# Projection slabs stepped in among attention tiles, and two attention runs joined, in a three-layer transformer kernel

## The chip, the cores and the metric

The kernel runs on one core of a Trainium2 chip. The metric is the device time of one execution in microseconds (us). TensorE (PE) does the matrix products, VectorE (DVE), ScalarE (ACT) and GpSimd (POOL) work on 128 partitions, SyncE (SP) issues the weight loads. PSUM, the memory into which TensorE writes, has eight banks of 128 x 512 fp32 values.

## The reference, cut to what matters

512 tokens, width 1024, three layers in a row. Each layer is: norm, input projection, two mixers side by side of width 512, output projection, norm, gated FFN of width 2816.

```
layer 1: q,k,v, glu_a,glu_g = norm(x) @ w_in
         attn = block attention, 8 heads of 64, with a position bias     ("moba")
         conv = silu(layernorm(causal depthwise conv, 31 taps, of glu_a*sigmoid(glu_g)))
layer 2: fox:  8 heads of 64, logits + (c_q - c_k), c = cumsum(log_sigmoid(forget gate))
         diff: 4 heads of 128, softmax(q1 k1) - lambda * softmax(q2 k2), then an RMS norm per head
         q1,q2,k1,k2 of diff carry a partial rotary embedding
layer 3: latent ("dsa"): 8 heads, keys and values from a rank-128 latent; only the 128 keys of the
         largest index score count for a query (top-k)
         stick-breaking ("sb"): weights sigmoid(z) * product of sigmoid(-z) of later keys
x = x + concat(mixers) @ w_out;  x = x + ffn(norm(x));  after each layer's blocks a next norm
```

## The kernel before, in words

Everything is held transposed: features on partitions, 512 tokens along the row. Weights come in slabs of 128 x 2048 (a 1024 x 256 piece of a matrix), one load of 1 MB each into one of two slots `raw`, in one fixed order over the whole program; `BASE[phase]` is the number of a phase's first slab. Each slab is split into a high and a low part: ScalarE casts `w_hi` from `raw` (line 734), VectorE subtracts (`w_lo`, line 1075). TensorE multiplies each slab with the activations' parts `a_hi` and `a_lo` in three products: 48 matmuls of 512 columns for a feature slab (lines 368 to 370, 256 features), or 96 of 256 columns for a token slab (lines 381 to 383, values with tokens on partitions). The result stands in a pair of PSUM banks, pairs 0-1 and 2-3 in turn. `split(n + 2)` is done one slab ahead of its use.

Each engine has its own instruction list, written by hand in the order in which it runs; semaphores with counts tie them together (`wait("slab", n)` and so on). Nothing reorders them.

An attention stage consists of tiles: `Unit` u is one pair of heads (or one diff head) and one block of 128 queries `qt` (0 to 3), whose width is `u.w` = 128, 256, 384 or 512 keys. Layer 1 has 16 tiles, layers 2 and 3 have 32 (diff then fox; sb then dsa). `attend` on each engine runs rounds i, with the scores three tiles ahead (`AHEAD = 3`):

- TensorE (line 560): `scores(run[i+3])` (line 501) into a PSUM pair, `turn(run[i])` (transposes, line 520, banks 4 and 5), `values(run[i-1])` (line 537, banks 6 and 7 in turn by group of four tiles). Four `rotate` pairs and the root transposes `token_rows` stand in layer 2's projection.
- VectorE: `taken(run[i+3])` (line 1306) reads scores from PSUM, adds mask or bias and finds the row maximum; `factors(run[i+2])` (lines 1326 to 1337) scales by 1/sum; then spare work (`taps` of the convolution, line 1252, in layer 1; `top_rounds` in layer 3); then the eviction of a finished group (`a_lo`, line 1362). For sb tiles it is two scans (line 1315) and products (line 1320) in place of both.
- ScalarE: `exps(run[i+3])` (line 881), `move(run[i])` (line 903) copies the transposes out of PSUM, then the eviction's high part (`a_hi`, line 933) and the diff head's norm (lines 926 to 948).
- GpSimd, for fox only: adds the decay row to a tile's mask (lines 334 and 338), two tiles ahead.

Scores use two PSUM pairs in turn by the tile's number, so `scores(u)` waits for `taken` of the tile two before. All slabs of an input projection (10, 13, 11 in the three layers) are finished before a layer's `attend` begins, since the scores use the same banks. In layer 3 `attend` is called twice, for sb and for dsa; the masks of the chosen keys (lines 1610 and 1612) are made between them. In layer 1, VectorE does ten taps per projection slab from the fifth on (3 before the split, 7 behind it) and three per tile; 124 in all, which the layer norm's sums on TensorE (line 595) wait for.

Of the kernel before, what the change touches and what calls it, by code (L numbers as in the profile page):

```python
# [29 lines left out]
P = 128  # L30
S = 512
# [111 lines left out]

def runs_of(t):

    return [UNITS[t][i:i + 16] for i in range(0, len(UNITS[t]), 16)]
# [28 lines left out]
def build(nc, weights, vectors, x_in, positions, bias_rows, buckets, uk, uv,  # L175
# [4 lines left out]
    with ctx:  # L180
# [48 lines left out]
        fg = tmp[0:HEADS, 1:4, :]  # L229
# [17 lines left out]
        def lane_scores(u, lane):  # L247
            return ps[:, 2 * (u.n % 2) + lane, 0:u.w]
# [100 lines left out]
        def _(pe):  # L349
# [106 lines left out]
            def token_rows():  # L456

                for t in range(QT):
                    m = pe.transpose(ps[:, 6, t * P:(t + 1) * P], tmp[:, 5, t * P:(t + 1) * P], ident)
                m.then_inc(sem["rtok_mm"], 1)  # L460
# [29 lines left out]
            def scores(u):  # L490
                q = slice(u.qt * P, (u.qt + 1) * P)
                if u.n >= 2:
                    wait("taken", 2 * (u.n - 1))
                for lane in range(2):
# [28 lines left out]
            def values(u):  # L523
                wait("pt", 2 * u.n + 2)
                if u.first and u.group >= 2:
                    wait("oev", u.group - 1)
                q = slice(u.qt * P, (u.qt + 1) * P)
# [55 lines left out]
            for j in range(10):  # L583
                project("in1", j, in_fill("norm0") if j == 0 else None, tokens=j >= 8)
# [5 lines left out]
            wait("qkv", 6)  # L590
            attend(runs_of(1)[0])
# [32 lines left out]
            for j in range(1, 6):  # L624
                project("in2", j)
            wait("r23_dve", 2)
            wait("lam_act", 1)
            token_rows()
            wait("fg_dve", 4)
            for t in range(QT):  # L630
                m = pe.transpose(ps[:, 7, t * 8:t * 8 + 8], fg[:, 1, t * P:(t + 1) * P],
                                 sq_f[0:HEADS, 1, 0:HEADS])
            m.then_inc(sem["cq_mm"], 1)
            for j in range(6, 10):
                project("in2", j, tokens=j >= 9)
                for r in (2 * (j - 6), 2 * (j - 6) + 1):
                    wait("qkv", QKV["in2"] + j)
                    rotate(2, r, 8 + r)
            for j in range(10, 13):
                project("in2", j, tokens=True)  # L640
            wait("qkv", QKV["in2"] + 13)
            wait("rope", 8)
            wait("cq_ev", 1)
            attend(UNITS[2])
# [27 lines left out]
            token_rows()  # L672
# [40 lines left out]
            attend(runs_of(3)[0])  # L713
            attend(runs_of(3)[1])
# [6 lines left out]
        def _(act):  # L721
# [183 lines left out]

            def out_chunk(u):
# [3 lines left out]
            def attend(run):  # L910
                n, kind = len(run), run[0].kind
                ends = {i: u for i, u in enumerate(run) if u.last}
                for i in range(-AHEAD, n + 6):
                    a = i + AHEAD
                    if a < n:
                        if run[a].kind == "sb":
                            sticks(run[a])
                        else:
                            exps(run[a])
                    norms = {k: ends[i - k] for k in (2, 4, 6) if i - k in ends and ends[i - k].kind == "diff"}  # L920
                    if 4 in norms:
                        u = norms[4]
                        wait("df_sum", u.p + 1)
                        if u.p:
                            wait("alo", LOWS["att2"] + u.p)
                        A.activation(tmp[:, 1, :], ps[:, BT + 1, :], ACT.Ln, bias=col("eps"),
# [3 lines left out]
                    if i - 2 in ends and ends[i - 2].kind != "diff":  # L930
                        u = ends[i - 2]
                        wait("pv", u.n + 1)
                        A.copy(a_hi[:, out_chunk(u), :], ps[:, BO + u.group % 2, :]).then_inc(sem["ahi"], 1)
                    if 2 in norms:
                        u = norms[2]
                        wait("pv", u.n + 1)
                        if u.p:
                            wait("df_sum", u.p)
                        A.activation(tmp[:, 0, :], ps[:, BO + u.group % 2, :], ACT.Square
                                     ).then_inc(sem["df_sq"], 1)  # L940
                    if 4 in norms:
                        u = norms[4]
                        wait("df_ln", u.p + 1)
                        A.activation(tmp[:, 1, :], tmp[:, 1, :], ACT.Exp, scale=-0.5).then_inc(sem["df_root"], 1)
                    if 6 in norms:
                        u = norms[6]
                        wait("oev", u.group + 1)
                        A.copy(a_hi[:, out_chunk(u), :], tmp[:, 1, :]).then_inc(sem["ahi"], 1)
# [805 lines left out]
```

## Time and profile before

| | |
|---|---|
| median of 3 runs | 1937.97 us (1933.84 to 1938.27) |
| the profiled execution | 1936.62 us |
| its span, from the first to the last instruction | 1934.8 us |
| TensorE busy | 1834.5 us, 95% |
| VectorE, ScalarE, GpSimd busy | 1107.6, 753.6, 113.4 us |
| mean granted TensorE clock | 0.978 |
| moved from HBM | 163.10 MB, 85 GB/s over the span |

A clock of 1.00 is 2.4 GHz, 0.50 is 1.2 GHz; in between a stretch had both. A window row gives a stretch in us from the span's start, and in it each engine's busy time. A timeline row gives start, duration, engine, line, operation, tensors, and in brackets how long the engine was idle before it and what ended that. `x10` at the end of such a row means ten instructions merged, the time from the first's start to the last's end. PEld is the loading of the stationary operand, beside PE.

### The profile page before, as it was taken

To read this page: it belongs to the slowest core of one execution; us is meant where nothing else is said; L and a number is where in the kernel's file an instruction comes from. 1 tells how busy PE (TensorE), PEld (TensorE's weight loads), DVE (VectorE), ACT (ScalarE), POOL (GpSimd) and SP (SyncE) were. 2 spreads that over 40 slices of the span, in tenths; PEclk is the share of its full clock that TensorE was granted. 3 is DMA by queue.
4 is the path that set the end of the run, shared out by engine and by line. 5 is a ranking of instruction groups with operands and counts; after the bars stand their busy time and mean duration, and the time that the engine had idled before them with its cause. 6 is when DMAs were issued, how large, how long until landed. Compare 5 with 4: busy or idle time off the path is not lost.

```text
span 1934.8 us, 23475 instructions
## 1 busy us (share of the span) xinstructions
PE 1834.5 (95%) x8886; PEld 1466.6 (76%) x8886; DVE 1107.6 (57%) x1664; ACT 753.6 (39%) x1089; POOL 113.4 (6%) x114
## 2 busy tenths in 40 slices
PE   5987999999999999879999999999978999999998
PEld 4874788888887888448888888887755788888886
DVE  5889454444333454853667673347997366676422
ACT  4225443333323211663454442222257354445321
POOL 0000010000011000261000000100000010000000
PEclk9997999999999999889999999999989999999999
DMA  4430122223233422001322223332210123232221
GB/s 156 149 108 2 32 100 93 102 88 107 87 109 109 145 90 78 16 1 66 105 91 94 101 89 106 109 119 75 78 44 1 44 88 108 87 103 92 100 96 65
DMA packets 25719, 166.24 MB, mean 86 GB/s; under 512 B 3082, under 2 KB 3210, under 8 KB 6704
## 3 DMA queue, kind: packets, MB, share of 16 engines
q1 hardware_dynamic: 23328, 158.83, 23.8%
q0 software_dynamic: 1744, 5.37, 0.9%
q8 instruction: 50, 0.82, 0.2%
q10 hardware_dynamic: 576, 1.05, 0.2%
q14 instruction: 21, 0.17, 0.0%
HBM read 163.10 MB, written 2.13 MB: 85 GB/s over the span
## 4 chain that ended last, share of the span: by engine, by line
PE 88%; DVE 6%; issue 2%; ACT 2%; POOL 1%; DMA 0%; DVEq 0%; SPq 0%; ACTq 0%
PE ps L368 25%; PE ps L369 25%; PE ps L370 25%; PE ps L383 2%; PE ps L382 2%; PE ps L381 2%; PE ps L520 1%; PE ps L537 1%; DVE cacc L1252 1%; ACT ring L881 1%; DVE ring L1306 1%; PE ps L501 1%; POOL tmp L334 1%; PE ps L486 1%; DVE tmp L1315 1%
## 5 line engine op out<-in xcount | busy, mean ns | idle before, releaser
L368 PE MATMUL ps<-a_hi,w_hi 128*128 128x512 f32 x1616 | 635.3, 393 | 7.4 <-DVE a_lo L1081 3.8
L370 PE MATMUL ps<-a_hi,w_lo 128*128 128x512 f32 x1616 | 629.7, 390 | 0.0
L369 PE MATMUL ps<-a_lo,w_hi 128*128 128x512 f32 x1616 | 629.5, 390 | 0.0
L368 PEld LDWEIGHTS ps<-a_hi,w_hi 128*128 128x128 f32 x1616 | 303.9, 188 | 76.8 <-issue 9.8
L369 PEld LDWEIGHTS ps<-a_lo,w_hi 128*128 128x128 f32 x1616 | 304.0, 188 | 64.8 <-issue 2.6
L370 PEld LDWEIGHTS ps<-a_hi,w_lo 128*128 128x128 f32 x1616 | 303.8, 188 | 63.8
L1075 DVE TENSOR_TENSOR w_lo<-raw,w_hi 128x2048 fp32r<-128x2048 f32 x82 | 192.3, 2345 | 244.1 <-ACT w_hi L734 244.0
L734 ACT CAST w_hi<-raw 128x2048 fp32r<-128x2048 f32 x82 | 156.0, 1903 | 417.0 <-PE ps L370 335.1
L368 PE MATMUL ps<-h_hi,w_hi 128*128 128x512 f32 x528 | 206.2, 391 | 0.0
L370 PE MATMUL ps<-h_hi,w_lo 128*128 128x512 f32 x528 | 205.4, 389 | 0.0
L369 PE MATMUL ps<-h_lo,w_hi 128*128 128x512 f32 x528 | 205.4, 389 | 0.0
L1169 DVE TENSOR_TENSOR tmp<-ps,tmp 128x512 f32<-128x512 f32 x66 | 45.7, 692 | 175.1 <-PE ps L370 158.2
L1220 DVE SCALAR_TENSOR_TENSOR tmp<-tmp,vec 128x510 f32<-128x510 f32 (+1 forms) x176 | 120.0, 745 | 0.0
L369 PEld LDWEIGHTS ps<-h_lo,w_hi 128*128 128x128 f32 x528 | 99.1, 188 | 21.1 <-issue 0.5
L368 PEld LDWEIGHTS ps<-h_hi,w_hi 128*128 128x128 f32 x528 | 99.1, 188 | 20.9 <-issue 0.5
L370 PEld LDWEIGHTS ps<-h_hi,w_lo 128*128 128x128 f32 x528 | 99.1, 188 | 20.6
L1209 DVE TENSOR_TENSOR w_lo<-raw,w_hi 128x2048 fp32r<-128x2048 f32 x44 | 100.9, 2293 | 21.6 <-ACT w_hi L858 19.7
L520 PE MATMUL ps<-sq_f,ring 128*128 128x128 f32 x360 | 66.8, 317 | 46.8 <-ACT pT L903 32.4
L520 PEld LDWEIGHTS ps<-sq_f,ring 128*128 128x128 f32 x360 | 45.6, 160 | 84.7 <-DVE ring L1331 44.5
L858 ACT CAST w_hi<-raw 128x2048 fp32r<-128x2048 f32 x44 | 84.2, 1914 | 47.0 <-PE ps L370 47.0
L881 ACT ACTIVATE ring<-ring,stat 128x128 f32<-128x128 f32 (+3 forms) x128 | 70.8, 554 | 70.7 <-DVE stat L1306 70.6
L501 PE MATMUL ps<-qk 64*128 64x128 f32 (+3 forms) x320 | 75.5, 560 | 16.3 <-DVE stat L1306 9.5
(207 smaller groups left out, 1962.5 us busy)
## 6 DMA issues: line engine op xcount, KB each, us to landing
raw<-weights_dram SPq DMA_DIRECT2D x148, 1024.0 KB, 4.9
bias_t<-bias_rows_scratch POOLq DMA_DIRECT2D x8, 256.0 KB, 7.3
ncb<-decay_rows_scratch POOLq DMA_DIRECT2D x8, 256.0 KB, 4.7
out_dram<-xT SPq DMA_DIRECT2D x8, 256.0 KB, 2.0
xT<-x_in_dram ACTq DMA_DIRECT2D x4, 256.0 KB, 6.2
xT<-x_in_dram SPq DMA_DIRECT2D x4, 256.0 KB, 9.1
vec<-vectors_dram SPq DMA_DIRECT2D x1, 282.5 KB, 3.6
ring<-ramp_dram POOLq DMA_DIRECT2D x1, 260.0 KB, 5.4
```

The costliest lines, as they stand in the source:

```text
L368: pe.matmul(dst, wh, hi[:, k0 + k, :], start=start and k == 0, stop=False)
L369: pe.matmul(dst, wh, lo[:, k0 + k, :], start=False, stop=False)
L370: last = pe.matmul(dst, wl, hi[:, k0 + k, :], start=False, stop=stop and k == nk - 1)
L501: m = pe.matmul(lane_scores(u, lane), qq, kk, start=True, stop=u.kind != "sb")
L520: m = pe.transpose(ps[:, BT + lane, b * P:(b + 1) * P], e[:, b * P:(b + 1) * P], ident)
L734: A.copy(w_hi[:, n % 2, :], raw[:, n % 2, :]).then_inc(sem["whi"], 1)
L858: A.copy(w_hi[:, n % 2, :], raw[:, n % 2, :]).then_inc(sem["whi"], 1)
L881: A.activation(e, e, ACT.Exp, bias=stat[:, slot, 0:1], scale=-1.0, accum_out=stat[:, slot, 1:2]).then_inc(sem["ex"], 1)
L1075: Vv.tensor_tensor(w_lo[:, n % 2, :], raw[:, n % 2, :], w_hi[:, n % 2, :].bitcast(F32), ALU.subtract).then_inc(sem["wlo"], 1)
L1169: Vv.tensor_tensor(tmp[:, first, :], ps[:, bank + first, :], tmp[:, 5, :], ALU.mult).then_inc(sem["evg"], 1)
L1209: Vv.tensor_tensor(w_lo[:, n % 2, :], raw[:, n % 2, :], w_hi[:, n % 2, :].bitcast(F32), ALU.subtract).then_inc(sem["wlo"], 1)
L1220: step = Vv.scalar_tensor_tensor(out=to, in0=tmp[:, g, 0:S - lag], scalar=w, in1=to, op0=ALU.mult, op1=ALU.add)
```

## The change

The last three slabs of layer 1's input projection (numbers 7, 8, 9) and the last seven of layer 2's (6 to 12) are no longer done ahead of the attention but in steps of an eighth of a slab, `filler`, two (at two places three) in each round of TensorE's `attend`, between `scores` and `turn`, from round -3 on: to round 8 in layer 1, to round 23 in layer 2. Slabs are put in another order, so that what the first tiles need comes first (values with heads 0 to 3 of layer 1 as slab 6; in layer 2 diff before fox). The steps write into PSUM pair 2-3; as long as they do, and for the tiles whose scores are made then (`shared`), scores have only pair 0-1, so `scores(u)` waits for `taken` of the tile just before. A finished filler slab is moved out of PSUM, and the slab two further is split, in the round in which its last step stands (`FILLED`: rounds 0, 4, 8; in layer 2 also 12, 16, 20, 23). Because the steps still read the activations `a_hi` and `a_lo`, the finished attention groups may not be written there until round 9 (layer 1) or 24 (layer 2); diff results are parked in qk2 chunks 8 to 11 and copied in rounds 26, 27, 28 and 30. Layer 1 has ten taps fewer at each of three slabs and four in place of three per tile, the rest behind the last eviction. In layer 3 both runs become one `attend(UNITS[3])`: the masks and ScalarE's table load stand ahead of the first dsa tile's `taken` and `exps`.

```diff
+def filler_steps():
+    plan, step = {}, 0
+    for i in range(-AHEAD, 24):
+        count = 2 if i < 21 or i == 23 else 3
+        plan[i] = [(6 + (step + k) // 8, (step + k) % 8) for k in range(count)]
+        step += count
+    return plan
+STEPS = filler_steps()
+FILLED = {i: steps[-1][0] for i, steps in STEPS.items() if steps[-1][1] == 7}
+TOKENS = {"in1": (6, 9), "in2": (5, 6, 9, 12)}
+STEPS1 = {i: [(7 + k // 8, k % 8) for k in (2 * (i + AHEAD), 2 * (i + AHEAD) + 1)] for i in range(-AHEAD, 9)}
+FILLED1 = {i: steps[-1][0] for i, steps in STEPS1.items() if steps[-1][1] == 7}
+ALONE1 = 10 + AHEAD
+ALONE = 16 + 24 + AHEAD
+LATER = {26: 0, 27: 1, 28: 2, 30: 3}
...
-        fg = tmp[0:HEADS, 1:4, :]
+        fg = tmp[0:HEADS, 2:5, :]
+        r23 = tmp[:, 1, :]
...
-            return ps[:, 2 * (u.n % 2) + lane, 0:u.w]
+            pair = 0 if shared(u) else u.n % 2
+            return ps[:, 2 * pair + lane, 0:u.w]
+        def shared(u):
+            return u.n < {1: ALONE1, 2: ALONE, 3: 0}[u.t]
+        def evicted(run, i):
+            hold = {1: 9, 2: 24, 3: 0}[run[0].t]
+            return [u for k, u in enumerate(run) if u.last and u.kind != "diff" and max(k + 2, hold) == i]
...
             def scores(u):
                 q = slice(u.qt * P, (u.qt + 1) * P)
-                if u.n >= 2:
+                if u.n >= 1 and shared(u):
+                    wait("taken", 2 * u.n)
+                elif u.n >= 2:
                     wait("taken", 2 * (u.n - 1))
...
+            def filler(name, j, step):
+                n = BASE[name] + j
+                if step == 0:
+                    wait("wlo", n + 1)
+                    wait("qkv", QKV[name] + j - (4 if name == "in1" else 0))
+                if j not in TOKENS[name]:
+                    last = feature_major(n % 2, 2, a_hi, a_lo, step, 1, step == 0, step == DC - 1, at=step)
+                else:
+                    t, dst = step // 2, ps[:, 2 + step // 4, (step // 2 % 2) * 256:(step // 2 % 2) * 256 + 256]
+                    for k in range(step % 2 * 4, step % 2 * 4 + 4):
...
+                if step == 7:
+                    last.then_inc(sem["slab"], 1)
-            def attend(run):
+            def attend(run, steps={}):
                 n, kind = len(run), run[0].kind
                 for i in range(-AHEAD, n + 4):
                     if i + AHEAD < n:
                         scores(run[i + AHEAD])
+                    for j, step in steps.get(i, ()):
+                        filler(f"in{run[0].t}", j, step)
                     if 0 <= i < n:
                         turn(run[i])
...
-            for j in range(10):
-                project("in1", j, in_fill("norm0") if j == 0 else None, tokens=j >= 8)
+            for j in range(7):
+                project("in1", j, in_fill("norm0") if j == 0 else None, tokens=j >= 6)
...
-            wait("qkv", 6)
-            attend(runs_of(1)[0])
+            attend(UNITS[1], STEPS1)
...
-            attend(UNITS[2])
+            attend(UNITS[2], STEPS)
...
-            attend(runs_of(3)[0])
-            attend(runs_of(3)[1])
+            attend(UNITS[3])
...
@@ ScalarE, attend @@
                     if 0 <= i < n:
                         move(run[i])
-                    if i - 2 in ends and ends[i - 2].kind != "diff":
-                        u = ends[i - 2]
+                    if i in filled and run[0].t == 1:
+                        move_first(filled[i], 1)
+                    if i in filled:
+                        split(BASE[f"in{run[0].t}"] + filled[i] + 2)
+                    for u in evicted(run, i):
...
@@ VectorE @@
+            def filled_slab(j):
+                if j in TOKENS["in2"]:
+                    move_tokens("in2", j, v2, {6: 768, 9: 0, 12: 256}[j], pair=1)
+                else:
+                    c = {7: 0, 8: 4, 10: 2, 11: 6}[j]
+                    move_features("in2", j, qk2[:, c:c + 2, :], SCALE if c < 4 else 1.0, pair=1)
+                split(BASE["in2"] + j + 2)
...
                     if a < n and run[a].kind != "sb":
+                        if run[a] is runs_of(3)[1][0]:
+                            latent_masks()
                         taken(run[a])
...
                         spare()
-                    if i - 2 in ends and ends[i - 2].kind != "diff":
-                        u = ends[i - 2]
+                    if i in filled and run[0].t == 2:
+                        filled_slab(filled[i])
+                    elif i in filled:
+                        split(BASE["in1"] + filled[i] + 2)
+                    for u in evicted(run, i):
...
-            attend(runs_of(1)[0], lambda: taps(3))
+            attend(UNITS[1], lambda: taps(4), FILLED1)
+            taps(4 * TAPS)
...
-                if 1 <= j <= DC:
-                    c = j - 1
+                for c in range(2 * j - 2, 2 * j) if 1 <= j < 5 else ():
                     Vv.scalar_tensor_tensor(out=xT[:, c, :], in0=xT[:, c, :], scalar=col("gain", DC * 2 + c),
                                             in1=tmp[:, 0, :], op0=ALU.mult, op1=ALU.mult).then_inc(sem["x"], 1)
```

## Rows read from the trace of the kernel before

**Rows 1.** The page, 40 equal slices: TensorE's granted clock in tenths

```profile
PEclk9997999999999999889999999999989999999999
```

**Rows 2.** Windows: the attentions of layers 1, 2 and 3 (two runs)

```profile
core 0: us, PE busy (x) PEld busy (x) DVE busy (x) ACT busy (x) POOL busy (x), PEclk, DMA share, GB/s
...
136.40:203.06 66.66, 45.39 (x306) 28.39 (x305) 58.84 (x160) 35.32 (x102) 0.00 (x0) 0.77 0.05 17
...
767.05:871.00 103.95, 77.37 (x497) 47.21 (x497) 74.29 (x238) 66.84 (x198) 42.15 (x42) 0.87 0.03 11
...
1412.90:1467.95 55.05, 42.35 (x337) 25.00 (x337) 52.14 (x105) 38.33 (x101) 0.00 (x0) 0.88 0.06 20
...
1467.95:1514.65 46.70, 37.58 (x306) 23.19 (x304) 30.69 (x121) 33.77 (x103) 0.00 (x0) 0.93 0.01 1
```

**Rows 3.** Windows: dense slabs; four diff tiles; four latent tiles

```profile
300.00:320.00 20.00, 20.00 (x90) 16.57 (x89) 9.05 (x9) 6.71 (x7) 0.00 (x0) 1.00 0.30 105
...
797.94:808.16 10.22, 8.14 (x49) 4.89 (x48) 8.42 (x29) 7.81 (x23) 0.00 (x0) 1.00 0.01 2
...
1488.58:1498.70 10.12, 8.62 (x79) 5.43 (x77) 7.21 (x30) 7.62 (x26) 0.00 (x0) 1.00 0.00 1
```

**Rows 4.** Timeline of VectorE, layer 1

```profile
129.22 6.71 DVE L1252 SCALAR_TENSOR_TENSOR cacc<-cu,vec,cacc 128x512 f32<-128x512 f32 x10
...
138.53 2.29 DVE L1075 TENSOR_TENSOR w_lo<-raw,w_hi 128x2048 fp32r<-128x2048 f32 x1 [2.59 <-ACT w_hi L734]
...
163.74 0.68 DVE L1306 CUSTOM_DVE_ANT_0 ring<-ps,bias_t 128x512 f32<-128x512 f32 x1
...
203.79 0.69 DVE L1362 TENSOR_TENSOR a_lo<-ps,a_hi 128x512 fp32r<-128x512 f32 x1 [5.11 <-ACT a_hi L933]
```

**Rows 5.** Timeline of ScalarE and TensorE, layer 1

```profile
102.69 1.91 ACT L734 CAST w_hi<-raw 128x2048 fp32r<-128x2048 f32 x1 [8.04 <-PE ps L370]
...
136.60 1.90 ACT L734 CAST w_hi<-raw 128x2048 fp32r<-128x2048 f32 x1 [8.70 <-PE ps L383]
...
138.40 1.01 ACT L986 COPY v<-ps 128x1024 f32<-128x1024 f32 x1
...
145.93 3.36 PE L501 MATMUL ps<-qk 64*128 64x384 f32 x8 [5.02 <-DVE stat L1306]
...
203.06 3.70 PE L595 MATMUL ps<-cacc,sq_f 128*128 128x512 f32 x8
```

**Rows 6.** Windows: start of layer 1's attention

```profile
140.00:150.00 10.00, 4.98 (x18) 1.82 (x16) 9.57 (x29) 3.88 (x13) 0.00 (x0) 0.50 0.31 105
```

**Rows 7.** Timeline of VectorE (slab moves) and TensorE, layer 2

```profile
680.40 1.22 DVE L1264 SCALAR_TENSOR_TENSOR qk<-ps,tmp 128x1024 f32<-128x1024 f32 x1 [5.93 <-PE ps L370]
...
704.96 1.23 DVE L1264 SCALAR_TENSOR_TENSOR qk<-ps,tmp 128x1024 f32<-128x1024 f32 x1 [3.72 <-PE ps L370]
...
767.09 1.23 DVE L1271 TENSOR_TENSOR v<-ps,small 128x1024 f32<-128x1024 f32 x1 [7.24 <-PE ps L383]
...
771.84 3.36 PE L501 MATMUL ps<-qk 64*128 64x384 f32 x8 [2.55 <-DVE stat L1306]
```

**Rows 8.** Timeline of VectorE, GpSimd and TensorE, layer 2's second half

```profile
822.10 1.72 DVE L1331 TENSOR_SCALAR ring<-ring,stat 128x512 f32<-128x512 f32 x2
...
844.32 3.14 POOL L334 TENSOR_SCALAR tmp<-ncb,cq_t 128x512 f32<-128x512 f32 x2
...
847.25 1.13 PE L501 MATMUL ps<-qk 64*128 64x512 f32 x4
...
862.68 0.88 DVE L1331 TENSOR_SCALAR ring<-ring,stat 128x512 f32<-128x512 f32 x2
...
870.96 0.50 PE L368 MATMUL ps<-a_hi,w_hi 128*128 128x512 f32 x1 [1.41 <-DVE a_lo L1362]
```

**Rows 9.** Timeline between layer 3's two runs

```profile
1468.67 1.28 ACT L1055 ACT_TABLE_LOAD   x1
...
1468.68 0.69 DVE L1362 TENSOR_TENSOR a_lo<-ps,a_hi 128x512 fp32r<-128x512 f32 x1 [2.54 <-ACT a_hi L933]
...
1470.76 3.24 PE L501 MATMUL ps<-qk 64*128 64x384 f32 x8 [1.88 <-DVE stat L1306]
```

More of the change, by code:

```diff
@@ L491, in scores @@
                 q = slice(u.qt * P, (u.qt + 1) * P)
-                if u.n >= 2:
+                if u.n >= 1 and shared(u):
+                    wait("taken", 2 * u.n)
+                elif u.n >= 2:
                     wait("taken", 2 * (u.n - 1))
+                if u.kind == "diff" and u.first:
+                    wait("rope", 5 + u.p)
+                if u.kind == "fox" and u.first and u.p % 2 == 0:
+                    wait("qkv", QKV["in2"] + (9 if u.p == 0 else 12))
+                if u.t == 1 and u.n in (0, 8, ALONE1):
+                    wait("qkv", {0: 3, 8: 5, ALONE1: 6}[u.n])
+                if u.t == 2 and u.n == ALONE:
+                    wait("qkv", QKV["in2"] + 13)
                 for lane in range(2):
@@ L526, in values @@
                     wait("oev", u.group - 1)
+                if u.t == 1 and u.m == 8:
+                    wait("qkv", 6)
+                if u.t == 2 and u.first and u.p % 2 == 0:
+                    j = {"diff": (6, 7), "fox": (10, 13)}[u.kind][u.p // 2]
+                    wait("qkv", QKV["in2"] + j)
+                if u.kind == "diff" and u.m == 0:
+                    wait("rtok", 1)
+                    wait("cq_ev", 1)
                 q = slice(u.qt * P, (u.qt + 1) * P)
@@ L904, in move, with move_first, attend @@
                            ).then_inc(sem["pt"], 2 if diff else 1)
+            def move_first(j, pair):
+                wait("slab", BASE["in1"] + j + 1)
+                bank = ps[:, 2 * pair:2 * pair + 2, :]
+                if j in TOKENS["in1"]:
+                    c = 0 if j == 6 else 256
+                    A.copy(v1[:, :, c:c + 256], bank.rearrange("p b (t c) -> p (b t) c", c=256)
+                           ).then_inc(sem["qkv"], 1)
+                else:
+                    c = {4: 0, 5: 4, 7: 2, 8: 6}[j]
+                    A.activation(qk1[:, c:c + 2, :], bank, ACT.Copy, scale=SCALE if c < 4 else 1.0
+                                 ).then_inc(sem["qkv"], 1)
             def out_chunk(u):
                 return (4 if u.kind in ("diff", "sb") else 0) + u.p
-            def attend(run):
+            def attend(run, filled={}):
                 n, kind = len(run), run[0].kind
@@ L918, in attend @@
                         else:
+                            if run[a] is runs_of(3)[1][0]:
+                                act.preload_act_table_set("natural_log_exp_and_others")
                             exps(run[a])
-                    norms = {k: ends[i - k] for k in (2, 4, 6) if i - k in ends and ends[i - k].kind == "diff"}
+                    norms = {k: ends[i - k] for k in (2, 4) if i - k in ends and ends[i - k].kind == "diff"}
                     if 4 in norms:
@@ L1414, in _ @@
             wait("rope_act", 3)
-            for j in range(10):
+            for j in range(7):
                 o = PAIR["in1"] + j
@@ L1462, in _ @@
             wait("lam_dve", 3)
[L1463 removed]
+            for j in range(6):
                 n, o = BASE["in2"] + j, PAIR["in2"] + j
```

151 lines of the change are left out of this document (71 added, 80 removed).

## The prediction

> **What bounds the kernel now.** I read the clock row of the page first. TensorE's granted clock is 10 tenths nearly everywhere and dips in three places [rows 1]; these are the three attention stages. The dense stages can't be moved: 90 matmuls fill 20.00 us completely at clock 1.00, 0.222 us each [rows 3], so a slab of 48 costs 10.7 us, and nothing but less work shortens it. A token slab (96 matmuls of half the width) is 11.5: from the cast behind slab 6 to that behind slab 9 are 33.9 us, one feature slab and two of these [rows 5].
>
> Then the windows of the attention stages. In layer 1 TensorE is busy 45.4 of 66.7 us at clock 0.77, in layer 2 77.4 of 104.0 at 0.87 [rows 2]. In layer 1 the bound is VectorE, 58.8 of 66.7 us: it does the convolution's taps between the tiles. In layer 2 nobody is full (DVE 74, ACT 67, POOL 42 of 104): a stage of waits. Four tiles cost TensorE 8.1 us (diff) or 8.6 (two lanes; the latent tiles stand for fox) where the clock is 1.00, and VectorE 8.4 and 7.2 [rows 3]. At full clock the 32 tiles of layer 2 are 4 x 8.1 + 4 x 8.6 = 67 us of TensorE, so some 37 of its 104 are idle or lost to the clock; in layer 1 16 tiles are 34, so 32 of 66.7. That is what slabs could fill.
>
> **Layer 1: three slabs (7, 8, 9) go among the tiles.** TensorE's work is only moved. With them go 3 weight splits (2.2 us of VectorE, 1.9 of ScalarE each), three moves out of PSUM (1.0 of ScalarE) and 30 taps of 0.66 us [rows 4, 5], since each projection step carried ten taps. VectorE is the bound, and its work is moved, not removed:
> - Slab 6 is now a token slab and ends 0.8 later, at 103.4. VectorE comes to the first tile 9.0 later, as before (cast 1.9, split 2.2, seven taps 4.6; TensorE's 5.02 us of idleness ending at 145.93 is this [rows 5]): 112.4.
> - Its work until the last tap: 58.8 in the stage, less 2.3 and seven taps (4.6) ahead of the tiles, makes 51.9. Plus 30 taps 19.9 and three splits 6.6: 78.4 [rows 2, 4].
> - Waits. Scores now have one PSUM pair, so each scores() waits for the tile just before, and TensorE puts two filler steps (2.7) between two scores: VectorE starves in the first three rounds, whose own work is 3.4 us in all, by 5.0. In a filled round the split waits for tile, move and cast on ScalarE: scores 1.1 + steps 2.7 + transpose 0.4 + copy 0.4 + move 1.0 + cast 1.9 = 7.5 after the round's start, while VectorE is done at 5.8: 1.7, then less, 4 for three. Together 9.
> - 112.4 + 78.4 + 9 = 199.8, where TensorE began the layer norm's sums at 203.06: 3 earlier. But three taps now stand behind the last eviction, and TensorE has waited some 7 us; before, after idle stretches of 3.0 and 5.0 us, the clock was 0.50 over the ten us [rows 6], with 3.4 us for scores that cost half of it at full clock [rows 5]. I charge 2 for the restart. **Layer 1: -1.** Ends: no waits -10, double waits +8.
>
> In filler rounds both engines are full: VectorE 27.3/4 + sixteen taps 10.6 + split 2.2 = 19.6 per four tiles, TensorE 8.6 + 10.7 = 19.3. So little can be caught up.
>
> **Layer 2: seven slabs (6 to 12) go among 27 rounds.**
> - Slab 5 ended at 680.4 [rows 7]. It is now a token slab (+0.6, a slab with its handing over being 10.9) with the root transposes and three rotation pairs ahead; transposes and one pair cost 24.6 - 2 x 10.9 = 2.8 [rows 7], two more pairs some 3.4: 687.2. A last pair: 688.9. The attention began at 767.1: 78 earlier.
> - Start-up: scores and two steps to 692.2. VectorE is free at 695.7 (behind slab 5: move 1.2, wait 0.8, split 2.2, two ropes 4.0, copy 0.2). Two more rounds of scores and steps, 7.7: 703.4. The clock falls after such a pause [rows 6], 3 more: round 0 begins at 706.5.
> - Rounds 0 to 23 at full clock: 50 steps (two token slabs but for six steps, a third) 68.6; tiles 4 x 8.1 + 2 x 8.6 + 1.0 = 50.8; in the seven filled rounds the next but one scores() waits for VectorE, which stands behind ScalarE's cast: taken() at 9.7 where TensorE comes at 8.6, 1.1 each, 7.7. Sum 127: 833.6. VectorE has only 8.4 + 3.4 of 19 us, so this part is TensorE's, and busy shares of 8.1 in 10.2 us kept the clock at 1.00 [rows 3].
> - Splits now run beside GpSimd's decay tiles (3.14 for two at full width), where two scalings by VectorE took 1.72 instead of 0.88 [rows 8]. No split ran beside them before: between 0 and one GpSimd instruction, 1.6, for each of four; nearest is the scaling's 0.8, on less than all: +2, 835.6.
> - Tail: from the scores of tile 27 (847.25) to the next projection (870.96) 23.7 [rows 8]; the held-back evictions (six pairs of 0.6 on each of ScalarE and VectorE) add 1.5 (0 to 4): 860.8.
> - At nothing: the residual's scaling, now two per step, and the ropes moved two slabs forward fit into VectorE's 5.93 idle us per slab [rows 7]; another tile for the roots, and the diff results parked in freed chunks of qk2, move no work. The weight loads keep their order on SP's queue and wait for the splits; with 20 us between splits in place of 11 none is late. Without that cover the scaling would cost 0.7 more per slab.
> - **Layer 2: -10.** Ends: without the waits, slow clock, contention and evictions -24; with them doubled +4.
>
> On the contention the Trainium skill ("SBUF — State Buffer", Who interferes with whom) says that a VectorE instruction with two SBUF inputs and a GpSimd one that reads SBUF exclude each other, and the split is of that kind. By it each of the four splits is held for up to a whole GpSimd instruction, which would make the +2 a +6; the 1.72 beside 0.88 agrees in kind.
>
> **Layer 3: one pipeline.** TensorE's last stick values ended at 1467.95; then 2.54 us of VectorE idleness, a table load of 1.28, 1.88 idle on TensorE and 3.24 for scores at half clock [rows 9]. Merged, scores and transposes of the latent tiles begin earlier, but VectorE's bound remains until its last scan (52.1 of 55.1 us busy [rows 2]), the masks (1.0) and the table load move ahead of ScalarE's copies of the last three stick tiles, and these hold up the transposes: by my walk through the rounds only 1 us, and 1.5 of slow clock. **-2.5**, ends 0 and -5. The order of the tail is as before.
>
> **Sum.** -1 - 10 - 2.5 = -13.5 against the profiled execution, 1936.6 us (span 1934.8 and 1.8 around it); it lies 1.4 below the median shown. 1936.6 - 13.5 = 1923.1, by the median 1924.5: **1924**.
>
> **Rivals.**
> - *The waits are absorbed* (VectorE catches up, the rounds overlap). For it: tiles run three rounds ahead, layer 2's VectorE has seven idle us in nineteen. Against: one score pair allows one round of slack. The free ends sum to -10 - 24 - 5 = -39, **1899**; anything below 1912 counts here.
> - *The clock.* Short pauses in every round keep it as low as in the stage before, 0.87. TensorE's 119 us of rounds 0 to 23 grow by 0.15, 18: **1942**, no change. For it: 0.77 and 0.87 [rows 2]; against: 0.80 busy at 1.00 [rows 3]. The Trainium skill ("TensorE: Matmul & The Clock Gate", A second HAM failure mode: psum-queue depth-cycling) says that short pauses between groups as PSUM banks are cycled make the clock swing; this rival is that rule.
> - *The steps hide nothing*: TensorE works in order, the steps stand ahead of transposes and values, and a tile's chain grows by all of it. Then the 78 and 33 us saved ahead are given back: **1938**. Against: the transposes have two rounds of slack.
> - *Slower: the single score pair.* Scores, taken() and the next scores become one chain, 0.7 + 0.8 + 0.3 of handing over = 1.8 us in each round where VectorE is a round late. Eight of the 39 rounds eat the 13.5; from twelve on it is slower. In layer 1's twelve and the seven filled of layer 2: 19 x 1.8 = 34, **1958**. For it: layer 1's VectorE is full. Against: behind the scores lie 2.7 us of steps for taken() to hide in.
>
> **Chances.** Forecast 0.60 (own range 1912 to 1932), absorbed 0.17, clock 0.09, hides nothing 0.07, slower 0.07. The range takes in both no-change cases, 1938 and 1942, and leaves out half of "absorbed" below (0.085), "slower" (0.07) and a little of the clock's case above: 1908 to 1942. 0.3%, 5.8 us, is about what a measurement of this kernel can tell from no change: faster (below 1932.2) 0.77, same 0.16, slower 0.07.
>
> **What would show it.** Layer 1: first scores near 106.5; VectorE without gaps but for about 5 us at the start and 1 to 2 at w_hi in filled rounds; a TensorE pause of about 7 before the layer norm's sums near 200. Layer 2: first scores near 689 instead of 768; about 5 us per filled round, clock 1.00 from 710 on; the output projection near 861. Layer 3: stretch 1412.9 to 1514.65, 101.8, down to about 99. Wrong I am if the clock dips in the rounds, if a split waits several us in the fox half, or if TensorE's pauses in layer 1 are not at the two ends.

## The result, and the profile after

The changed kernel takes 1924.1 us (median of 4, 1922.8 to 1925.7) where the kernel before took 1937.97; the ratio is 0.9934, with a 95% interval of 0.9916 to 0.9951. Forecast were 1924, in 1912 to 1932 for its own case. The total is right, but partly by luck: layer 1 came out 3.2 us worse than forecast and layer 2 3.0 better, and the two cancel. By the profiled executions (span 1934.8 before), with the start of each output projection as the mark:

| stage | before | after | measured | forecast |
|---|---|---|---|---|
| to layer 1's output projection | 206.19 | 208.37 | +2.2 | -1 |
| from there to layer 2's | 664.77 | 651.59 | -13.2 | -10 |
| from there to layer 3's | 643.69 | 641.23 | -2.5 | -2.5 |

The page after: span, busy time of each engine, and the granted clock in 40 slices, the row that answers to [rows 1].

```profile
span 1921.4 us, 23482 instructions
...
PE 1827.2 (95%) x8886; PEld 1461.7 (76%) x8886; DVE 1104.5 (57%) x1664; ACT 754.9 (39%) x1089; POOL 114.5 (6%) x114
...
PEclk9998899999999999989999999999989999999999
```

The three dips of the clock are narrower but still there. The windows show where; they answer to [rows 2]: the tiles of layer 1 with the three slabs among them, its layer norm sums, rounds 0 to 23 of layer 2, its tail, and three pieces of layer 3.

```profile
core 0: us, PE busy (x) PEld busy (x) DVE busy (x) ACT busy (x) POOL busy (x), PEclk, DMA share, GB/s
112.60:203.08 90.48, 67.98 (x481) 49.83 (x481) 78.95 (x182) 40.06 (x106) 0.00 (x0) 0.91 0.10 36
203.08:208.37 5.29, 5.29 (x8) 2.23 (x9) 0.00 (x0) 0.00 (x0) 0.00 (x0) 0.59 0.00 0
...
707.47:830.39 122.92, 119.21 (x737) 91.95 (x737) 70.21 (x185) 58.20 (x147) 33.36 (x33) 1.00 0.16 52
830.39:859.96 29.57, 20.48 (x159) 13.47 (x157) 18.51 (x47) 18.52 (x46) 9.89 (x9) 0.83 0.11 36
...
1401.92:1456.97 55.05, 42.52 (x312) 24.70 (x312) 53.95 (x116) 38.53 (x103) 0.00 (x0) 0.84 0.06 20
1456.97:1475.00 18.03, 14.49 (x132) 9.19 (x130) 12.91 (x55) 14.14 (x48) 0.00 (x0) 1.00 0.00 1
1475.00:1501.19 26.19, 21.32 (x202) 13.95 (x198) 15.74 (x57) 18.86 (x55) 0.00 (x0) 1.00 0.01 2
```

Layer 2's rounds are what the change is for: TensorE is busy 119.2 of 122.9 us at clock 1.00. The tail behind them is worse than before, 29.6 us at 0.83 where [rows 8] gave 23.7. In layer 1 VectorE is busy 79.0 of 90.5 us, and TensorE does its sums at clock 0.59.

The timeline of VectorE and TensorE in layer 1 (start, duration, and in brackets the idle time before and who ended it):

```profile
106.02 0.80 PE L542 MATMUL ps<-qk 64*128 64x128 f32 x4 [2.96 <-ACT v L975]
112.49 0.70 PE L542 MATMUL ps<-qk 64*128 64x256 f32 x4 [0.36 <-DVE stat L1378]
113.23 0.42 DVE L1378 CUSTOM_DVE_ANT_0 ring<-ps,bias_t 128x256 f32<-128x256 f32 x1 [0.79 <-PE ps L542]
117.02 0.56 DVE L1378 CUSTOM_DVE_ANT_0 ring<-ps,bias_t 128x384 f32<-128x384 f32 x1 [2.42 <-PE ps L542]
121.04 0.69 DVE L1378 CUSTOM_DVE_ANT_0 ring<-ps,bias_t 128x512 f32<-128x512 f32 x1 [2.25 <-PE ps L542]
127.31 2.29 DVE L1147 TENSOR_TENSOR w_lo<-raw,w_hi 128x2048 fp32r<-128x2048 f32 x1 [1.45 <-ACT w_hi L797]
147.87 2.29 DVE L1147 TENSOR_TENSOR w_lo<-raw,w_hi 128x2048 fp32r<-128x2048 f32 x1 [1.20 <-ACT w_hi L797]
168.76 2.29 DVE L1147 TENSOR_TENSOR w_lo<-raw,w_hi 128x2048 fp32r<-128x2048 f32 x1 [1.49 <-ACT w_hi L797]
177.81 0.42 DVE L1378 CUSTOM_DVE_ANT_0 ring<-ps,bias_t 128x256 f32<-128x256 f32 x1 [1.49 <-PE ps L542]
...
195.06 5.38 DVE L1324 SCALAR_TENSOR_TENSOR cacc<-cu,vec,cacc 128x512 f32<-128x512 f32 x8
200.35 0.69 DVE L1448 TENSOR_TENSOR a_lo<-ps,a_hi 128x512 fp32r<-128x512 f32 x1
200.95 2.07 DVE L1324 SCALAR_TENSOR_TENSOR cacc<-cu,vec,cacc 128x512 f32<-128x512 f32 x3
203.08 5.86 PE L664 MATMUL ps<-cacc,sq_f 128*128 128x512 f32 x8 [8.56 <-DVE cacc L1324]
```

First scores at 106.0 (forecast 106.5). VectorE starves for 0.79 + 2.42 + 2.25 = 5.5 us in the three start-up rounds (forecast 5.0) and waits 1.2 to 1.5 for each cast, 4.1 in three (forecast 4). Eleven taps stand at the end, three of them behind the last eviction; TensorE waits 8.56 us for them and then takes 5.86 us for sums that took 3.70 in [rows 5].

The same for layer 2, with two of TensorE's short pauses in filled rounds (behind `taken()`, and behind VectorE's normalised result, which frees a bank for the values), GpSimd around one split, and the end of the filled rounds:

```profile
691.04 0.49 PE L542 MATMUL ps<-qk 64*128 64x128 f32 x4
...
698.40 0.70 PE L542 MATMUL ps<-qk 64*128 64x256 f32 x4 [3.81 <-DVE stat L1378]
...
735.19 0.70 PE L542 MATMUL ps<-qk 64*128 64x256 f32 x4 [0.23 <-DVE stat L1378]
...
775.10 0.46 PE L586 MATMUL ps<-pT,v 128*128 128x128 f32 x2 [0.82 <-DVE qk L1453]
...
790.43 0.67 POOL L369 TENSOR_TENSOR tmp<-tmp,causal 128x256 f32<-128x256 f32 x1
792.18 2.29 DVE L1147 TENSOR_TENSOR w_lo<-raw,w_hi 128x2048 fp32r<-128x2048 f32 x1 [1.21 <-ACT w_hi L797]
...
795.65 1.53 POOL L365 TENSOR_SCALAR tmp<-ncb,cq_t 128x384 f32<-128x384 f32 x1 [4.54 <-DVE stat L1378]
...
832.22 2.29 DVE L1147 TENSOR_TENSOR w_lo<-raw,w_hi 128x2048 fp32r<-128x2048 f32 x1 [2.17 <-ACT w_hi L797]
835.15 0.72 ACT L944 ACTIVATE ring<-ring,stat 128x512 f32<-128x512 f32 x1 [2.97 <-DVE stat L1378]
836.97 1.09 PE L561 MATMUL ps<-sq_f,ring 128*128 128x128 f32 x4 [3.63 <-ACT pT L966]
...
859.96 0.50 PE L399 MATMUL ps<-a_hi,w_hi 128*128 128x512 f32 x1 [1.41 <-DVE a_lo L1448]
```

The attention starts at 691.0, which is the forecast 688.9 plus the 2.2 that layer 1 lost. The last split (832.22) belongs to the seventh slab and feeds the second slab of the output projection, which TensorE reaches some 36 us later (859.96 and a slab of 10.7). It waits 2.17 us for ScalarE and runs 2.29. Behind it come the tile's `taken()`, ScalarE's exponential (2.97 idle) and TensorE (3.63 idle); from 835.5 to 842.3 the clock is at half (1.09 us for four transposes that take 0.63 at full clock).

### The profile page after: what moved, and what is told of

It reads as the page before. It is cut to its first block, busy times and chain, and to the rows that moved or that the text cites. A ratio compares the mean times of both kernels' runs of the same rounds, so it can differ in the third digit from the quotient of the medians.

```text
span 1921.4 us, 23482 instructions
## 1 busy us (share of the span) xinstructions
PE 1827.2 (95%) x8886; PEld 1461.7 (76%) x8886; DVE 1104.5 (57%) x1664; ACT 754.9 (39%) x1089; POOL 114.5 (6%) x114
## 4 chain that ended last, share of the span: by engine, by line
PE 88%; DVE 5%; ACT 3%; issue 3%; DMA 0%; DVEq 0%; SPq 0%; ACTq 0%
PE ps L399 25%; PE ps L401 25%; PE ps L400 25%; PE ps L542 2%; PE ps L561 1%; DVE cacc L1324 1%; PE ps L586 1%; ACT w_hi L797 1%; PE ps L622 1%; ACT ring L944 1%; PE ps L414 1%; PE ps L413 1%; PE ps L412 1%; PE ps L623 1%; PE ps L624 1%
## 5 line engine op out<-in xcount | busy, mean ns | idle before, releaser
L944 ACT ACTIVATE ring<-ring,stat 128x128 f32<-128x128 f32 (+3 forms) x128 | 71.0, 556 | 119.2 <-DVE stat L1378 119.2
L399 PEld LDWEIGHTS ps<-h_hi,w_hi 128*128 128x128 f32 x528 | 99.1, 188 | 21.1 <-issue 0.5
L400 PEld LDWEIGHTS ps<-h_lo,w_hi 128*128 128x128 f32 x528 | 99.1, 188 | 21.0 <-issue 0.5
L401 PEld LDWEIGHTS ps<-h_hi,w_lo 128*128 128x128 f32 x528 | 99.1, 188 | 20.6
L934 ACT ACTIVATE tmp<-tmp 128x512 f32<-128x512 f32 x44 | 27.8, 632 | 157.7 <-DVE tmp L1292 157.7
L339 POOL TENSOR_TENSOR tmp<-tmp 128x512 f32<-128x512 f32 x28 | 36.8, 1316 | 872.7 <-ACT tmp L810 871.0
L561 PE MATMUL ps<-sq_f,ring 128*128 128x128 f32 x360 | 59.6, 295 | 28.0 <-ACT pT L966 21.2
```

The source lines that it names most:

```text
L399: pe.matmul(dst, wh, hi[:, k0 + k, :], start=start and k == 0, stop=False)
L400: pe.matmul(dst, wh, lo[:, k0 + k, :], start=False, stop=False)
L401: last = pe.matmul(dst, wl, hi[:, k0 + k, :], start=False, stop=stop and k == nk - 1)
L561: m = pe.transpose(ps[:, BT + lane, b * P:(b + 1) * P], e[:, b * P:(b + 1) * P], ident)
L944: A.activation(e, e, ACT.Exp, bias=stat[:, slot, 0:1], scale=-1.0, accum_out=stat[:, slot, 1:2]).then_inc(sem["ex"], 1)
```

## The experiments

Eleven kernels ran in four groups, each beside runs of the kernel before (medians 1936.9 to 1937.4 us). Edits are to the changed kernel unless said; `...` marks lines left out. Times of whole kernels are medians; marks, windows and waits come from one profiled execution each.

One thing limits what a single mark tells. Behind the same pause TensorE's half clock can begin and end at another place in another execution. Layer 1's output projection, 208.37 in the changed kernel, stands at 209.31 in u_l3 and 210.57 in e_defer, whose layer 1 is the same code. In e_defer the start-up's half clock lasted from 110.8 to 117.7 us, in the changed kernel from 105.1 to 111.9, and VectorE's longest wait for scores in the start-up was 4.59 us in place of 2.42. A difference of 2 us at this mark is within the scatter of equal code.

**One part undone: layer 1** (u_l1). All ten slabs come ahead of the tiles; the slab loops of all three engines change alike, and the first scores wait for the last key slab.

```
-STEPS1 = {i: [...] for i in range(-AHEAD, 9)}
+STEPS1 = {}
...
-ALONE1 = 10 + AHEAD
+ALONE1 = 0
...
-            hold = {1: 9, 2: 24, 3: 0}[run[0].t]
+            hold = {1: 0, 2: 24, 3: 0}[run[0].t]
...
-            for j in range(7):
+            for j in range(10):
...
-            attend(UNITS[1], lambda: taps(4), FILLED1)
+            attend(UNITS[1], lambda: taps(3), FILLED1)
```

> The changed kernel with its layer 1 part undone: all ten slabs of layer 1 run before the first tile, two score pairs, three taps per tile; only the new order of layer 1's slabs stays. Theory from the two traces: layer 1's part costs 2.2 us, so this kernel is 2.2 us faster than the changed one, about 1922 against 1924, and TensorE's layer norm sums begin about at the same 203 us, with the output projection some 2 us earlier. Rival (the forecast's own term): layer 1's part gains 1 us, so this kernel is 1 us slower. Layers 2 and 3 as in the changed kernel under both.

Measured: 1923.2 us (1920.6 to 1924.2), 0.9 less than the changed kernel, and the output projection at 206.45, 1.9 earlier. So layer 1's part cost 1.9 us at that mark (2.9 and 4.1 against the marks of u_l3 and e_defer). Even so the two profiled executions took the same time, 1923.2: layer 3, with the same code, took 2.1 us longer in this one.

**One part undone: layer 3** (u_l3). `attend(UNITS[3])` is two calls again, `attend(runs_of(3)[0])` and `attend(runs_of(3)[1])`, on all three engines.

> The changed kernel with its layer 3 part undone: the stick-breaking and the latent tiles of layer 3 are two pipelines again, one after the other. Theory: merging them gave 2.5 us, so this kernel is 2.5 us slower than the changed one and TensorE shows the 2.5 us of idleness before the first latent scores again. Rival: the 2.5 us came from elsewhere in the layer (the clock of the last tiles), and undoing costs under 1 us.

Measured: 1924.6 us (1924.0 to 1927.6), 0.5 more. TensorE's pause before the latent scores is back (1.88 us at 1460.70), and yet the stretch from layer 2's output projection to layer 3's is only 0.5 us longer, 641.69. The theory fell. The clock in the 18 us behind the stick values differs between executions, which is where the rest of the 2.5 lies. First u_l3 (two pipelines):

```profile
1457.90:1475.90 18.00, 13.98 (x103) 7.85 (x102) 14.24 (x64) 14.34 (x46) 0.00 (x0) 0.91 0.00 1
```

and u_l1 (merged as in the changed kernel), window and a row of its timeline:

```profile
1454.97:1473.00 18.03, 15.77 (x124) 9.81 (x120) 10.99 (x46) 12.16 (x38) 0.00 (x0) 0.84 0.00 1
```

```profile
1456.47 1.94 PE L561 MATMUL ps<-sq_f,ring 128*128 128x128 f32 x8 [0.76 <-ACT pT L966]
```

In the changed kernel the same eight transposes came at full clock, in 1.06 us. Up to 1454 the two executions agree row by row, shifted by 2.0; then the full clock returned some 6 us later in u_l1. Over all traces the stretch from layer 3's last move of v to its output projection took 99.1 to 99.2 us in six merged executions and 100.8, 101.2 and 101.7 in three more (c_all, u_l1, e_last); with two pipelines it took 99.7 in one and 101.4 to 101.7 in three, the kernel before among them. Where the half clock falls is worth some 2 us either way. The merging is worth about 0.5 by the shortest stretches, which the medians can't tell from nothing. Whether merging makes the short stretch likelier (six of nine against one of four) so few executions can't say.

**Taps into the start-up** (e_taps).

```
                     if 0 <= i < n:
                         spare()
+                    elif i < 0 and run[0].t == 1:
+                        taps({-3: 1, -2: 3, -1: 3}[i])
```

> The changed kernel with VectorE's taps spread anew in layer 1: one, three and three taps in the three start-up rounds, where VectorE starved for 0.8, 2.4 and 2.3 us, so that none is left behind the last eviction. Theory (VectorE's work plus its waits set the end of layer 1, as the forecast summed it): the seven taps, 4.65 us, go into idleness, the layer norm's sums begin 4 to 5 us earlier, and the kernel is 4.6 us faster; with TensorE's pause ahead of the sums shortened by as much, up to 2 us more from the clock. Rival (the taps do not set the end, the last tiles' chain of exponentials, transposes and values does): the sums begin under 1.5 us earlier.

Measured: 1917.2 us (1915.7 to 1918.1), 6.9 less. VectorE's waits in layer 1 (total, times, longest; those for scores were 6.9 in four in the changed kernel):

```profile
DVE w_lo L1147 <- ACT w_hi L797: 4.2, 3, 1.5
...
DVE ring L1378 <- PE ps L542: 2.2, 3, 1.5
```

and the end of the stage:

```profile
195.19 2.73 DVE L1324 SCALAR_TENSOR_TENSOR cacc<-cu,vec,cacc 128x512 f32<-128x512 f32 x4
...
197.98 3.70 PE L664 MATMUL ps<-cacc,sq_f 128*128 128x512 f32 x8 [1.55 <-DVE cacc L1324]
```

The sums begin 5.1 us earlier, their pause is 1.55 in place of 8.56, and they run at full clock: 2.16 more. The theory holds with both its terms, the taps and the clock; the output projection starts at 201.11, 7.3 earlier, more than the scatter of 2.2.

**The last filled split behind the attention** (e_defer), on ScalarE as shown and on VectorE alike; the added call stands behind the loop over rounds.

```
-                    if i in filled:
+                    if i in filled and filled[i] != 12:
                         split(BASE[f"in{run[0].t}"] + filled[i] + 2)
...
+                if run[0].t == 2:
+                    split(BASE["in2"] + 14)
```

> The changed kernel, but the weight split that follows the last filled slab of layer 2 (1.9 us of ScalarE and 2.2 of VectorE in round 23) is put behind the attention, where TensorE already runs the output projection. Theory: this split is what made the tail of layer 2 29.6 us instead of 25.2, since it holds up the tiles behind it and with them the clock: 3 to 5 us faster. Rival: the tail is long because of the held-back evictions in its rounds, whose place is not changed here: under 1 us.

Measured: 1922.0 us (1919.1 to 1923.1), 2.1 less; its layer 1 happened to end 2.2 later than in the changed kernel, and its layer 2 took 648.27, 3.3 less. The window of the tail:

```profile
832.75:858.84 26.09, 18.34 (x158) 12.11 (x156) 16.05 (x46) 16.70 (x45) 10.52 (x9) 0.93 0.00 1
```

26.1 us at 0.93 in place of 29.6 at 0.83: 3.5 of the tail's excess of 5.9 over [rows 8] was this split and its clock. The edit gave the same 3.3 in layer 2 on top of e_taps (652.26 to 648.99 in c_taps_defer). What is left, 2.4, may be the held-back evictions (forecast 1.5), the seventh slab's move, or both; no run separates them.

**VectorE's split one round behind the cast** (e_late), in both layers.

```
             def filled_slab(j):
...
-                split(BASE["in2"] + j + 2)
...
-                    elif i in filled:
-                        split(BASE["in1"] + filled[i] + 2)
+                    if i - 1 in filled:
+                        split(BASE[f"in{run[0].t}"] + filled[i - 1] + 2)
```

> The changed kernel, but VectorE's part of the weight split comes one round behind ScalarE's cast in both layers, so that VectorE no longer stands at the cast in filled rounds (1.1 to 1.5 us each in layer 1, 1.1 to 2.2 in layer 2). Theory (these waits are part of VectorE's sum in layer 1 and TensorE's waits in layer 2): layer 1 ends 4 us earlier, layer 2's rounds 0 to 23, 122.9 us now, shrink by up to 3.7, together 4 to 7 us faster. Rival (VectorE's time is only moved: it waits in the next round for scores instead, as one score pair allows no lead): under 1.5 us.

Measured: 1915.9 us (1915.7 to 1918.2), 8.2 less: 2.8 in layer 1 and 4.3 in layer 2 by the marks, and layer 3's stage as long as before to 0.02. VectorE's waits in layer 1, and layer 2's rounds and tail:

```profile
DVE ring L1378 <- PE ps L542: 8.7, 7, 2.4
```

```profile
704.68:824.53 119.85, 118.67 (x737) 91.86 (x736) 71.26 (x185) 58.27 (x147) 39.19 (x33) 1.00 0.16 54
824.53:852.90 28.37, 20.83 (x158) 13.83 (x157) 19.24 (x47) 18.61 (x46) 11.94 (x9) 0.82 0.11 38
```

The waits at the cast are gone. In layer 1 some came back as waits for scores (8.7 in place of 6.9), as the rival had it, so the sums begin 2.5 us earlier and not 4.1. In layer 2 TensorE fills 118.7 of 119.9 us: the rounds have nothing left to give.

In this kernel the four splits of the fox half run beside GpSimd's decay tiles, which they never did in the changed kernel. The first of them:

```profile
767.95 4.95 POOL L365 TENSOR_SCALAR tmp<-ncb,cq_t 128x384 f32<-128x384 f32 x2 [68.31 <-DVE stat L1378]
...
769.59 2.29 DVE L1147 TENSOR_TENSOR w_lo<-raw,w_hi 128x2048 fp32r<-128x2048 f32 x1
```

The split takes its usual 2.29 us. GpSimd's pair of instructions takes 4.95, where the same pair took 2.83 in the changed kernel; its second instruction began 0.4 us before the split and was held all the same. The other three splits took 2.27 or 2.28, beside pairs of 4.46, 4.75 and 3.89. So the two do exclude each other, and each time it is GpSimd that waits. TensorE doesn't: its only pauses over 0.15 us in rounds 0 to 23 are 0.88 and 0.17, both behind a slab's move.

**Steps behind the values** (e_last): TensorE's order in a round.

```
-                    for j, step in steps.get(i, ()):
-                        filler(f"in{run[0].t}", j, step)
                     if 0 <= i < n:
                         turn(run[i])
                     if 1 <= i <= n:
                         values(run[i - 1])
+                    for j, step in steps.get(i, ()):
+                        filler(f"in{run[0].t}", j, step)
```

> The changed kernel, but the two projection steps of a round stand behind the round's transposes and values on TensorE instead of ahead of them. Theory (the transposes have two rounds of slack, so the place of the steps in the round is free, and the tiles' chain is not lengthened by them): within 1.5 us of the changed kernel. Rival (steps hide nothing, they lengthen each tile's chain by 2.7 us): faster by more than 5 us, as the chain is shorter by them here. A third: behind the values, the steps no longer cover taken() between two scores, and each round pays: slower by 5 us or more.

Measured: 1958.8 us (1956.3 to 1959.1), 34.7 slower, 30.2 of it in layer 2. Theory and rival both fell; it is the third case (slower by 5 us or more), but `taken()` is not what TensorE waits for. Two windows, then two rows of TensorE and one of VectorE:

```profile
750.00:770.00 20.00, 15.71 (x94) 13.12 (x94) 10.02 (x24) 6.66 (x17) 0.00 (x0) 0.83 0.16 54
770.00:790.00 20.00, 15.67 (x94) 12.80 (x93) 10.78 (x24) 8.08 (x19) 3.50 (x3) 0.85 0.16 54
```

```profile
781.88 2.29 DVE L1147 TENSOR_TENSOR w_lo<-raw,w_hi 128x2048 fp32r<-128x2048 f32 x1 [0.76 <-ACT w_hi L797]
784.98 0.77 PE L586 MATMUL ps<-pT,v 128*128 128x128 f32 x2 [4.33 <-DVE qk L1453]
...
811.09 0.50 PE L586 MATMUL ps<-pT,v 128*64 128x128 f32 x4 [4.07 <-issue]
```

A slab ends, and TensorE comes at once, behind scores and transposes of 0.9 us, to the first values of the next head pair. These wait for VectorE's normalised result (L1453), which frees their PSUM bank and stands behind the slab's move and split. In the changed kernel the next two steps, 2.7 us of work, lie in between, and so do a tile's transposes and values; its longest pause there is 0.82 us (775.10). Behind each of the three pauses of over 4 us the clock is at half, and the steps take nearly twice as long. From 710 to 862, near the end of the seventh slab, TensorE is busy 130.8 us and idle 21.2; in the changed kernel's rounds 0 to 23 it was 119.2 and 3.7.

**The single score pair alone** (e_pair), on the kernel before.

```
-            return ps[:, 2 * (u.n % 2) + lane, 0:u.w]
+            return ps[:, 2 * (u.n % 2 if u.t == 3 else 0) + lane, 0:u.w]
...
+                if u.n >= 1 and u.t < 3:
+                    wait("taken", 2 * u.n)
```

> The kernel before the change with one thing of it alone: layers 1 and 2 have one pair of PSUM banks for scores, so that each tile's scores wait until VectorE has taken the tile just before. No steps are among the tiles. The rival 'slower: the single score pair' at 1.8 us a round gives 48 rounds x 1.8 = 86 us more than before. Theory: the chain of scores, taken and scores is paid only where nothing else stands between them; VectorE's taps (layer 1) and its scalings cover most of it: 4 us more than before, 0 to 15.

Measured: 1943.8 us (1943.6 to 1946.6), 6.4 more than the kernel before (ratio 1.0037, 1.0023 to 1.0050): +3.9 at layer 1's mark, +3.5 in layer 2. TensorE's own waits at scores in layer 1, which were 5.0 us, once, in the kernel before:

```profile
PE ps L503 <- DVE stat L1308: 13.2, 10, 6.0
```

That is 0.13 us for each of 48 rounds, not 1.8. The chain exists (the waits went from 5.0 to 13.2), but the mark moved by 3.9 alone. The likely reason is that VectorE's scalings and taps run beside it; this run has no steps among the tiles, so it prices the pair alone.

**The edits together** (c_taps_defer, c_all).

> Both edits that gave time, together on the changed kernel: taps in layer 1's start-up rounds, and the last filled split of layer 2 put behind the attention. In the traces the one took 7.3 us off layer 1 (208.37 to 201.11 at the first output matmul) and the other 3.3 off layer 2 (651.59 to 648.27). Theory: they add, 10.6 off 1923, about 1913 by the profiled spans. Rival: the clock gives part of it back in the new tail: 1916 to 1917.

Measured: 1913.4 us (1911.9 to 1915.2), 10.7 less than the changed kernel: they add (marks 10.6, medians 6.9 + 2.1).

> The changed kernel with all three edits that gave time: taps in layer 1's start-up rounds, VectorE's part of each filled split one round behind the cast, and the last filled split of layer 2 behind the attention. By the stage marks of the single runs: layer 1 ended at 208.37 in the changed kernel, 201.11 with the taps, 205.59 with the late splits; if both sum, 198.3. Layer 2 took 651.59 from there, 648.27 with the deferred split, 647.31 with the late ones, which already move that split by a round: 645 to 647. Theory (VectorE's sum in layer 1): 1921.4 - 10.1 - 5 = 1906 of span, 1908 us. Rival (with the taps spread, the end of layer 1 is set by the last tiles and not by VectorE's sum, so the late splits give nothing there): 1911 us.

Measured: 1909.2 us (1907.2 to 1910.9); to the kernel before 0.9854 (0.9837 to 0.9870), the fastest kernel of the study and 14.9 us below the changed one. Layer 1 ends at 200.65 and so gains only 0.5 from the late splits once the taps are spread (rival right); layer 2 takes 645.48, as forecast.

**Is each part still worth it in that kernel?** c_all with layer 1's part undone, and c_all with layer 3 as two pipelines:

> As the kernel with all three edits, but layer 1's part of the change undone: no projection steps among layer 1's tiles, taps as before. It tells what layer 1's part is worth once VectorE starves less: its layer 1 should end at about 206.4, as it did with that part undone before. Theory: layer 1's part is then worth 6 to 8 us, so this kernel takes 1914 to 1917. Rival: the gain seen with the taps came from elsewhere, and both kernels are within 2 us.

> As the kernel with all three edits, but layer 3's two attentions are two pipelines again. In the traces so far the stretch from layer 3's last move of v to its output projection took 99.2 us merged in four executions, 101.3 and 100.8 merged in two others, and 99.7 and 101.8 with two pipelines, so the clock's return after the pause moves it by about 2 us whatever the code. Theory (the merging itself is worth 0.5 us, the rest of the 2.5 was the clock): within 1.5 us of the merged kernel's 1909.2. Rival (the forecast's 2.5): 1911.7 or more.

Measured: 1917.4 us (1913.8 to 1917.8) without layer 1's part, so it is now worth 8 us by the medians and 4.1 at its own mark (204.75 to 200.65; the profiled execution was the fastest of the four). The mark was expected at 206.4, where u_l1 with the same layer 1 had it; the 1.7 between them is scatter again, so 4 to 6 us is what the marks support. With two pipelines in layer 3 it takes 1909.3 (1909.0 to 1911.4), 0.1 apart from the merged kernel.

## Why the prediction was right, and where its terms were off

**Layer 1: mechanism right, sum too small by 3.** VectorE's work plus its waits does set the end: e_taps took seven taps, 4.65 us, out of the sum, and the sums began 5.1 earlier. Forecast were 78.4 + 9 us from 112.4; measured 79.5 busy, 11.0 of waits and 0.6 of small gaps, from 111.9. The start-up (5.5 for 5.0) and the waits at the cast (4.1 for 4) were as computed; missing were 1.5 for one late score (177.81) and 1.1 of busy time. Of that, 0.7 is the last eviction: it now stands ahead of the last taps (200.35), while in the kernel before it came behind the start of the sums (203.79 [rows 4]). There VectorE had done its last tap by 196.6 and then waited 5.11 us for the last tiles [rows 4], so it was not VectorE that set the end of the stage before; it sets it now. The restart at half clock, charged at 2, cost 2.16. So the -1 became +2.2 (up to 4.4 in the other executions of this code), and the part of the change in layer 1 was a small loss as it stood.

**Layer 2: start right, rounds too dear, tail too cheap.** The rounds' work, 68.6 + 50.8 = 119.4, was measured at 119.2. The waits in filled rounds were put at 7.7 and were 3.7, and they were others: the forecast had `scores()` wait 1.1 us for `taken()` in each of seven rounds, while only two such pauses of over 0.15 us show, 0.25 and 0.23. Most of the rest stands at the first values of a group, which need their bank (0.64, 0.82 and 0.60), and behind a slab's move (0.88 and 0.16). The +2 for splits beside GpSimd was 0: those of the second half took 2.29 us like the others, since the decay tile that GpSimd does next waits for the `taken()` behind the split (795.65, 4.54 idle), so the two never met. By the Trainium skill ("SBUF — State Buffer", Who interferes with whom) the term would have been 6. In e_late, where they did meet, the exclusion that it states is there, but GpSimd was held and not the split, and layer 2 still got 4.3 us shorter. The tail was forecast at 25.2 and took 29.6: the step that failed is the one that charged it with the held-back evictions alone and put the seventh slab's split among the rounds, at 1.1; its cast and split in the tail cost 3.5 us with the clock (e_defer). With 1.2 less in the start-up, 6 less in the rounds and 4.4 more in the tail, the -10 became -13.2.

**Layer 3: right by luck.** The merging gives about 0.5 (u_l3 +0.5, c_all_no3 +0.1), and not the 1 us of earlier transposes with 1.5 of clock behind it; the rest of the -2.5 was where the half clock fell in the two profiled executions, which moves this stage by 2 us whatever the code.

**The rivals.** *The clock* stayed away: 1.00 over rounds 0 to 23, with 97% of TensorE busy. The Trainium skill ("TensorE: Matmul & The Clock Gate", A second HAM failure mode: psum-queue depth-cycling) has short pauses between groups, as PSUM banks are cycled, make the clock swing. The short pauses of the changed kernel (none over 0.9 us in rounds 0 to 23) did not do so; e_last's pauses of over 4 us at a PSUM bank did, down to 0.83 over 20 us. *The single pair* costs 0.13 us a round alone. *The steps hide nothing*: e_last shows that they do more than fill, they are the cover for VectorE's slab work. *Waits are absorbed* was partly true, in layer 2 alone (3.7 of 7.7 us left).

## What to carry to other kernels

Where filler work goes among the tiles of an attention, look first at what the fillers themselves ask of the other engines (moves, casts, splits) and at which instruction stands right behind it: the same steps two places later cost 35 us. Then put spare work where the new schedule starves an engine, here seven taps into three start-up rounds (6.9 us), and move what nobody needs soon (the last split) out of the tail. A long pause of TensorE costs twice, by itself and by the clock after it. Where two kernels differ by 2 us at a mark close to such a pause, compare several executions before naming a cause.

## What the runs showed of the hardware that was not expected

- The same instructions with the same pauses (up to 1.75 us, layer 3's merged tiles) were at half clock for 3.4 us in one execution and 10.2 in another, and got the full clock back about 6 us apart, which moved the stage by 2.1 us. A difference of that size in one profiled execution is no proof of an effect of an edit.
- Eight float matmuls of 512 columns took 3.70 us after a pause of 1.55 us (e_taps), 5.86 after one of 8.56, and 6.28 after one of 6.54 (u_l3): the price of the restart does not grow with the pause.
- A weight split of VectorE (two inputs in SBUF) beside GpSimd's decay tiles kept its 2.28 us in all four cases of e_late, also where GpSimd had begun first; the GpSimd instruction then took up to 3.73 us, where none took over 1.65 in the changed kernel.
